# Two transformer blocks on one core: a second attention with another division of its work, expert loads behind other waits, mirrored slots, and products that nobody reads

## What is computed

```python
# block 1
x = x + mixed @ w_out                                  # convolution and dilated attention
x = x + memory_cross_attention(h, m, w_xq, w_xk, w_xv, w_xo)
x = x + hierarchical_moe(rms_norm(x), ...)             # MoE1: 32 experts, EXPERT_FF = 512
x = rms_norm(x, final_norm_g)
# block 2
z = rmsnorm(x) @ w_in                                  # q, k, v, f, u_ssm, g_attn, g_ssm
y_attn = forgetting_attention(q, k, v, f + b_forget)   # 8 heads of 64
y_ssm = s5(u_ssm, ...)
mixed = sigmoid(g_attn) * (y_attn @ w_proj_attn) + sigmoid(g_ssm) * (y_ssm @ w_proj_ssm)
x = x + mixed @ w_out
x = x + hier_moe(rmsnorm(x), ...)                      # MoE2: 32 experts, D_EXPERT = 256

def forgetting_attention(q, k, v, f_logit):            # per head, for each block of 128 queries
    logits = q @ k.T + F[t] - F[s]                     # F = cumsum(log_sigmoid(f))
    logits = where(s <= t, logits, -1e30)
    return softmax(logits) @ v

def moe(x):                                            # top-1 group of 4, then top-2 of its 8 experts
    y[token] = sum over its 2 experts of gate * ((silu(x @ w_gate[e]) * (x @ w_up[e])) @ w_down[e])
```

## Time and profile before

| | before |
|---|---|
| median of 3 runs | 1913.36 us (1911.27 to 1916.16) |
| profiled execution, its own time | 1914.55 us |
| its span in the trace | 1912.7 us |
| granted TensorE clock, mean | 0.948 |
| PE busy | 1652.7 us (86%) |
| DVE, ACT, POOL busy | 503.5, 328.6, 376.9 us |
| chain that ended last, by engine | PE 53%, DMA 30%, DVE 7%, POOL 4%, ACT 3% |
| DMA: moved, mean rate | 436.96 MB, 228 GB/s |

### The profile page before, as it was taken

The page is one execution under the profiler, slowest core; times in us unless marked ns, Lnnn a source line. Parts: engine busy times, 40 slices in busy tenths (PEclk is TensorE's granted clock), DMA queues, the critical chain, the costliest instruction groups (busy, mean ns, idle before and its releaser), DMA issues.

```text
span 1912.7 us, 18683 instructions
## 1 busy us (share of the span) xinstructions
PE 1652.7 (86%) x7098; PEld 807.8 (42%) x7098; DVE 503.5 (26%) x1203; ACT 328.6 (17%) x718; POOL 376.9 (20%) x360
## 2 busy tenths in 40 slices
PE   8999989989897887778777759999999997988775
PEld 4445456444544332222222225546644444544332
DVE  4565664110324301000000022513300015311110
ACT  3002541121311000000000020313300012111111
POOL 0122544881201111111110110020001001222222
PEclk9999999989997999989899969999999997998898
DMA  9123004412645999999999674940031245999993
GB/s 315 41 88 110 1 12 174 177 45 99 219 178 216 421 414 419 416 421 415 417 418 415 251 233 113 244 110 23 1 88 61 71 160 224 401 398 403 401 402 123
DMA packets 101718, 436.96 MB, mean 228 GB/s; under 512 B 15656, under 2 KB 23496, under 8 KB 75392
## 3 DMA queue, kind: packets, MB, share of 16 engines
q1 hardware_dynamic: 58896, 299.03, 41.0%
q10 hardware_dynamic: 24272, 105.99, 13.5%
q0 software_dynamic: 18464, 30.76, 6.1%
...
## 4 chain that ended last, share of the span: by engine, by line
PE 53%; DMA 30%; DVE 7%; POOL 4%; ACT 3%; issue 2%; SPq 1%; ACTq 0%; POOLq 0%; DVEq 0%
PE ps L261 27%; DMA ring<-in_w 19%; DMA ring<-in_w_expert_up 9%; PE ps L1763 8%; PE ps L1346 5%; PE ps L1779 2%; PE ps L2244 2%; DMA work<-hmid,rowtok 1%; PE ps L773 1%; PE ps L758 1%; SPq L1942 1%; PE ps L1372 1%; PE ps L732 1%; POOL ring L1106 1%; POOL ring L1107 1%
## 5 line engine op out<-in xcount | busy, mean ns | idle before, releaser
L1763 PE MATMUL ps<-ring,work 128*64 128x256 f32 (+1 forms) x1472 | 273.3, 529 | 74.3 <-DMA ring<-in_w 44.3
L261 PE MATMUL ps<-kept,ring 128*128 128x512 f32 x640 | 280.5, 598 | 2.9 <-DVE kept L1401 1.3
L1763 PEld LDWEIGHTS ps<-ring,work 128*64 128x64 f32 x1472 | 113.3, 150 | 238.3 <-issue 119.9
L261 PEld LDWEIGHTS ps<-kept,ring 128*128 128x128 f32 x640 | 122.2, 192 | 156.9 <-issue 153.9
L1881 DVE TENSOR_TENSOR work<-work,ps 128x256 f32<-128x256 f32 (+1 forms) x64 | 22.7, 354 | 629.0 <-ACT work L1840 608.2
L1779 PE MATMUL ps<-ring,work 128*64 128x512 f32 x544 | 129.5, 611 | 27.2 <-issue 26.2
L1763 PE MATMUL ps<-kept,work 128*64 128x512 f32 (+1 forms) x640 | 117.6, 524 | 30.4 <-DMA kept<-in_w 18.0
L1927 POOL DMA_INDIRECT hres<-work,rowdst x33 | 51.7, 1567 | 434.0 <-ACT work L1850 433.7
L261 PE MATMUL ps<-ring,kept 128*128 128x512 f32 (+1 forms) x320 | 124.7, 550 | 0.3 <-PE ps L261 0.3
L1346 PE MATMUL ps<-ring,kept 128*128 128x512 f32 x256 | 114.5, 602 | 1.7 <-ACTq L245 1.4
L1840 ACT ACTIVATE work<-ps 128x256 f32<-128x256 f32 (+1 forms) x64 | 21.1, 330 | 458.4 <-PE ps L1763 458.4
...
## 6 DMA issues: line engine op xcount, KB each, us to landing
...
```

The source lines that it names most:

```text
L261: last = nc.tensor.matmul(out_, l, r, start=i == 0, stop=i == len(pairs) - 1)
L1763: last = nc.tensor.matmul(ps[64 * hf:64 * hf + 64, bank, 0:ff].rearrange("p (w n) -> p w n", w=2), xT[:, k, :], up[:, :, k * ff + hf * hw: ...
```

## The change

**Second attention.** The mask product is gone from PE: POOL adds `causal` to `Fb` in a buffer (`bias2`), for each head of a pair one sum of 128 x 512 that masks every 128-column piece, and after block t has been read it copies the plain `Fb` back over piece t, so that the next block finds only its last piece masked. DVE reads `bias2` in place of `Fb`. The probabilities are normalised before they are turned: by POOL for t = 0 and 1, by ACT for t = 2 and 3. There are four buffers of them, and the lag on PE is 4 blocks. The copy of the transposes goes into a buffer for a whole pair of heads (`pTf`), and the product with v is done once for a pair: v as weights (64 columns), 512, 384, 256 and 128 columns of probabilities, 8 products where there were 20 for each pair. The output lands transposed; `turn_o2`, `o2` and ACT's L2668 are gone, and a copy of 128 x 512 for each pair on ACT comes in. The scores of blocks 0 to 3 stand ahead of the last tile of v, the copy of that tile stands behind the fourth exp on ACT, and the four groups of `ga` stand between the last transposes and products.

**Routes and norms.** `keep_busy(bank, n)` multiplies the identity by itself n times, 512 columns, and nobody reads the result: two in front of the waits of `turn(3)` in n5, n6 and n9, five ahead of the first turn of each `moe_pe`, 8 + 4 in `entry_pe`. In PE's list `lsum(2)` goes behind `turn(3)`, in DVE's `turned_dve(n, 3)` ahead of the choice for tile 2.

**Entry.** On DVE `gained(3)` and every `scale(t+1)` go ahead of `turned(t)`.

**Expert loads.** The loads of the last third of the places wait for the last logits, the last turn and the four writes of `hmid`, and no longer for the first gather. The first part of the load of expert 2 in MoE2 goes ahead of a wait. `over_gather` is issued four experts earlier.

**Slots.** `iota_slot` is permuted: within every 32 slots the upper 16 stand in reverse order, so that rank 16 is in slot 31 and rank 31 in slot 16.

```diff
+        def keep_busy(bank, n):
+            for _ in range(n):
+                nc.tensor.matmul(ps[:, bank, :].rearrange("p (a n) -> p a n", a=4), ident[:, :],
+                                 ident[:, :].unsqueeze(1).to_broadcast([P, 4, P]), start=True, stop=True)
...
             def turn(t):
-                pe.wait_ge(S(f"{n}_xn"), since(f"{n}_xn") + t + 1)
-                pe.wait_ge(S(f"{n}_xa"), since(f"{n}_xa") + t + 1)
                 if t >= 2:
                     pe.wait_ge(S(f"{n}_hd"), since(f"{n}_hd") + t - 1)
                     pe.wait_ge(S(f"{n}_ha"), since(f"{n}_ha") + t - 1)
+                if t == 3:
+                    keep_busy(2, 2)
+                pe.wait_ge(S(f"{n}_xn"), since(f"{n}_xn") + t + 1)
+                pe.wait_ge(S(f"{n}_xa"), since(f"{n}_xa") + t + 1)
...
+            keep_busy(0, 5)
             turn(0)
...
-                if e == NE - 4:
+                if e == NE - 8:
                     pool.wait_ge(S(f"planned{m}"), since(f"planned{m}") + 1)
                     pool.wait_ge(S(f"xturned{m}"), since(f"xturned{m}") + NE // 2 - 3)
                     over_gather(pool, m, rowtok[:, NE // 2:NE // 2 + 1])
...
+                load_up(2)
                 sp.wait_ge(S("w_used1"), since("w_used1") + 21)
-                for e in range(2, 4):
-                    load_up(e)
-                    load_down(e)
-            sp.wait_ge(S(f"xg{m}_0"), since(f"xg{m}_0") + 16)
+                load_down(2)
+                load_up(3)
+                load_down(3)
+            sp.wait_ge(S(f"logits{m}"), since(f"logits{m}") + T)
+            sp.wait_ge(S(f"n{m}_turned"), since(f"n{m}_turned") + T)
+            sp.wait_ge(S(f"hmid{m}"), since(f"hmid{m}") + 16 * T)
...
         def entry_pe(pe):
+            keep_busy(4, 8)
+            pe.wait_ge(S("xback_0"), since("xback_0") + 16)
+            keep_busy(4, 4)
...
             variances(1)
+            gained(3)
+            scale(1)
             turned(0)
-            scale(1)
-            gained(3)
...
-                    for m in range(2):
-                        n = (head1(i)[1] + 1) * P
-                        nc.tensor.matmul(ps[:, (i + m) % 4, n - P:n], ident[:, :], causal, start=False, stop=True
-                                         ).then_inc(S("f2_scores"), 1)
...
+                    for c in range(T):
+                        for m in range(2):
+                            last = nc.tensor.matmul(ps[64 * m:64 * m + 64, 6 + hp % 2, c * P:SEQ],
+                                                    v2[:, c, (2 * hp + m) * 64:(2 * hp + m) * 64 + 64],
+                                                    pTf(hp, m)[:, 512 * c:384 * c + 512], start=c == 0, stop=c == T - 1)
...
+            for hp in range(H2 // 2):
+                for k in range(8):
+                    i, t, m = 8 * hp + k, k // 2, k % 2
+                    pool.wait_ge(S("f2_masked"), since("f2_masked") + i + 1)
+                    if t < T - 1:
+                        nc.gpsimd.tensor_copy(bias2(hp, m)[:, t * P:t * P + P], Fb[:, 2 * hp + m, t * P:t * P + P]
+                                              ).then_inc(S("f2_bias"), 1)
+                    elif hp + 2 < H2 // 2:
+                        build(hp + 2, m)
+                    j = i - 1
+                    if k and by_pool(j):
+                        n = (j % 8 // 2 + 1) * P
+                        pool.wait_ge(S("f2_rden"), since("f2_rden") + j + 1)
+                        nc.gpsimd.tensor_scalar(prf(j)[:, 0:n], prf(j)[:, 0:n], rden[:, j:j + 1], None, ALU.mult
+                                                ).then_inc(S("f2_norm_pool"), 1)
...
-    putr("iota_slot", np.arange(P))
+    slot = np.arange(P)
+    putr("iota_slot", np.where(slot // 16 % 2 == 0, slot, slot // 16 * 16 + 15 - slot % 16))
```

202 lines of the change are left out of this document (117 added, 85 removed).

## The result

| | before | changed |
|---|---|---|
| median | 1915.17 us (5 runs) | 1904.28 us (5 runs) |
| ratio to before | 1 | 0.994, 95% interval 0.9918 to 0.9962 |
| profiled execution: time, span | 1914.55, 1912.7 | 1899.47, 1897.6 |
| granted clock, mean | 0.948 | 0.955 |

One of the five executions of the changed kernel took 3312.8 us and counts as slow: the ratio goes by the four others (median 1903.5 us).

A forecast was written before the change was run, and what follows sets the result against it. Weights' DMA was taken to bound both expert stages, PE the second attention, a three-engine loop the entry. Gains of 16 + 5 + 7.5 + 2.5 + 9 + 5 = 45 us from the median 1913.4 gave 1868, range 1856 to 1885.

The forecast's parts named there:

- 7.3 as a union: Second attention: PE's 9.0 us by line for a pair of heads shrink to 7.3 busy, as instructions overlap (factor 0.81).
- 1.17 times the work: Second attention: a pair's period exceeds PE's busy time as in the first attention, 15.66 us for 13.38.
- 9.4 us a pair: Second attention: the period forecast for a pair of heads, down from 12.75 us; gain 16 us.
- C: Rival, second attention: bound by its round trip through the engines, 12 us a pair, gain 5.8 not 16; 1878 us; chance 0.15.
- I take nothing: MoE1's start: the first gather sharing the DMA engines with the early load was counted as costing 0, bounded by 10 us.
- the clock comes back: MoE1's start: five unread products raise PE's clock earlier, so expert 3's load moves from 620.4 to some 617.5; gain 5 us.
- the step from the length of the fall to the map of engines: End of MoE1: the 13 us fall in DMA share fits partition p on engine p mod 16, spread 16 us; mirror gains 7.5.
- the map of four neighbouring slots: Expert stages: the Trainium skill's map, four neighbouring partitions to an engine; mirror would bring nothing; rejected, its spread being 34 us.
- B: Rival, expert stages: the mirrored slots balance nothing, engines being dealt otherwise than p mod 16; 1880.5 us; chance 0.12.
- the twelve unread products lie in PE's wait for the read-back: Entry of block 2: the unread products cost nothing and may lift PE's clock; the entry's gain 2.5 us.
- the rest: Unread products ahead of `turn(3)`, `lsum`, DVE's order in the choice, earlier overflow gather: counted 0; the products' range -2 to +3 us.
- D: Rival, expert stages: early loads starve the first gathers, landing 10 us later; both stages lose their 14 us; 1882; chance 0.03.

The follow-up runs named there:

- e6: The changed kernel with DVE's copy of block i-5's transposes placed ahead of the reciprocal of block i-1 in the second attention; 1894.6 us.
- e4: The changed kernel with the loads of the last third of the places waiting for the first gather again, as before the change; 1905.1 us.

## Why the prediction was wrong, point by point

**The reading of the bounds was right**: MoE1 and MoE2 by the weights, the attention by PE, the entry by a loop. It failed in what becomes late next.

**Attention: the steps "7.3 as a union" and "1.17 times the work", 9.4 us a pair, and C at 0.15.** The work of DVE, ACT and POOL was right to 0.5 us (POOL under its bound of 9), the period was 11.1 to 13.4. Two things were wrong. First, in the new kernel a loop through DVE, ACT and PE set the period, because of a reciprocal in the wrong place. I took the first attention's ratio of period to PE's busy time for a property of the scheme; it is one of a loop's order. That C held, with 9.0 of its 10 us (7.0 gained up to w_out in place of 16), and e6 showed the mechanism: with the order mended a pair takes 10.26, and the stretch up to w_out is 14.5 us below before. Second, the sum of PE's lines was nearly right, 9.5 us in e6 against 9.0, but not the factor of 0.81 for their overlap, which I had from the old loop: PE's union in e6 is 8.68 us and not 7.3. The mended loop takes 1.18 times that. So 9.4 was too low even without the ring; with 10.26 a pair my sum gives 12.8 and not 16, and the 14.5 come near 16 because the two ends gave more than I had counted.

**MoE1's start: the step "I take nothing" for the gather, and the step "the clock comes back".** The gather under load took 8.64 us, which is inside the bound of 10 that I had named and then set to zero. And the five products, which I had in the wait for the gather, ended 3.3 us ahead of it, because the gather came later; the clock fell again. The two errors are one: the wait's end moved, and everything laid into the wait was sized for its old end. Gain 5 forecast, -0.9 measured, which is none, as profiles of the same code differ by more.

**Mirrored slots: the step from the length of the fall to the map of engines.** A spread of 30 rows fitted the 13 us of the fall, one of 63 rows did not, and I took the fit for evidence against the map of four neighbouring slots. Wrong besides was the price of a row at the end: by this map dealing takes 24 rows off the fullest engine of MoE1, 13 us at 0.54 a row, and 7 were measured. A fall shorter than the spread and a gain smaller than the rows' price go together; that the lightly loaded engines spend part of their lead as idle time during the stage, since the ring lets no load start before a place is free, would explain both, but this is argued and not shown. B was the case, at 0.12.

**Entry: the step "the twelve unread products lie in PE's wait for the read-back", and their price.** The order was worth 2.5 to 2.7 us (2.5 forecast). The products cost 6.8 to 7.8, because most of the 16 us of idle were not a wait for data: PE is held until the last row addition and then clears 41 semaphores. Of the wait some 4 us are left, and twelve products take 13.5 us. Each takes 0.86 us at full clock and 1.71 at half in this run, start to start, and not the 0.46 and 0.92 of the prediction. The profile of before doesn't show this, since it puts all of PE's idle there down to what ended it last. The code does: the wait for POOL and the loop of clears stand right ahead of `entry_pe`. I read only the busy share.

**MoE2: 14 forecast, 5.5 measured.** The early loads gave 5.0 (e4), below the 6 to 11; the mirror nothing. As soon as the weights come early the gathers lead, in 15 to 16 us each, a wait that had come up once in the chain of before.

**Not foreseen**: 2.9 us gained in n5 and 3.1 in n6, n9 and the routes ("the rest", counted as 0 with a range up to +3), and 2.6 lost in s5: 1.1 in its first group (30.6 us against 29.5) and 1.4 in one that partly ran at the lower clock (last section).

**The range.** B, C and D's mechanism held together. I gave them 0.30 in sum as if one excluded the others, and set the upper end at the worst of them alone. They sit in different stages and add: 12.5 of B, 10 of C and 14 of D on 1868 give 1904.5. That was in my numbers and not in my range. That this sum meets the measured 1904.3 is luck: the early loads of MoE2 kept 5 of the 14 that D gives away and the norms gained 6, while the entry's products cost 7 and s5 2.6 that no rival has.
